# Border of the first two stages of an encoder block: seven weight splits move from VectorE to GpSimd, and the last sixteen tokens' turned tiles share one buffer behind the keys' products

## The reference

```
hn   = rmsnorm(h, attn_norm)
q_g, k_g, v_g, c_q, c_kv, k_r, gates = split(hn @ w_in)      # 512,128,128,384,256,32,2048 columns
q_g  = rope_2d(rmsnorm(q_g per head));  k_g = rope_2d(rmsnorm(k_g per head))
q_m  = rmsnorm(c_q) @ mla_w_uq           # 384 -> 8 heads of 64 + 32 rotated columns
kv   = rmsnorm(c_kv) @ mla_w_ukv         # 256 -> 8 heads of 64 key + 64 value columns
... grouped attention, latent attention, gates, w_out, experts, final norm
```

## Time and profile before

| | us |
|---|---|
| median of 3 runs | 2993.95 (2992.51 to 2995.31) |
| the profiled execution | 2994.37 |
| its span, first to last instruction | 2992.6 |
| TensorE busy in the span | 2826.5 (94%) |
| VectorE, ScalarE, GpSimd busy | 1820.7, 1479.4, 684.4 |

### The profile page before, as it was taken

How to read it: one execution, slowest core, us unless ns; L and a number is a source line. 1 busy time by engine, 2 the same in 40 slices (tenths; PEclk the granted TensorE clock), 3 DMA queues, 4 the chain that set the end, 5 groups by cost and what they waited for, 6 DMA issues and landing times. The chain is left out here.

```text
span 2992.6 us, 56058 instructions
## 1 busy us (share of the span) xinstructions
PE 2826.5 (94%) x20084; PEld 2619.8 (88%) x20084; DVE 1820.7 (61%) x3158; ACT 1479.4 (49%) x2701; POOL 684.4 (23%) x1247
## 2 busy tenths in 40 slices
PE   8999899999999999999999999999965999999994
PEld 7888698999998888887999999988844999999994
DVE  6777767888887777676334334433345555555555
ACT  4333336888887777677223223321222445544443
POOL 0000013444443333334000000000013233332331
PEclk9999898999999999999999999999976999999997
DMA  6556592202113224443757564456655898889977
GB/s 212 158 157 191 152 377 86 71 24 72 50 33 93 75 74 108 102 125 99 225 137 228 160 203 132 144 174 197 190 138 141 198 207 199 201 203 209 207 161 260
DMA packets 529044, 461.87 MB, mean 154 GB/s; under 512 B 53458, under 2 KB 464802, under 8 KB 528880
## 3 DMA queue, kind: packets, MB, share of 16 engines
q1 hardware_dynamic: 510256, 411.74, 48.0%
q0 software_dynamic: 16256, 47.89, 7.5%
q10 hardware_dynamic: 2368, 0.16, 0.0%
HBM read 315.57 MB, written 144.14 MB: 154 GB/s over the span
## 5 line engine op out<-in xcount | busy, mean ns | idle before, releaser
L1576 DVE TENSOR_REDUCE t_peak<-t_s_ps 128x1 f32<-128x1024 f32 (+2 forms) x276 | 336.8, 1221 | 84.8 <-PE t_s_ps L1388 83.9
L1388 PE MATMUL t_s_ps<-t_k,t_q 96*128 96x512 f32 (+2 forms) x1392 | 379.0, 402 | 4.8 <-ACT t_probs L1492 4.8
L1840 PE MATMUL c_acc<-c_tokens,c_w_hi 128*128 128x260 f32 x2048 | 373.0, 283 | 4.5 <-DVE c_w_lo L1913 4.5
L1601 DVE TENSOR_TENSOR t_pt_lo<-t_tp,t_pt_hi 128x512 fp32r<-128x512 f32 x552 | 336.4, 650 | 36.1 <-ACT t_pt_hi L1522 35.5
L1522 ACT CAST t_pt_hi<-t_tp 128x512 fp32r<-128x512 f32 x552 | 284.7, 565 | 113.0 <-PE t_tp L1418 112.0
L1840 PEld LDWEIGHTS c_acc<-c_tokens,c_w_hi 128*128 128x128 f32 x2048 | 316.8, 189 | 4.8 <-issue 4.8
L1492 ACT ACTIVATE t_probs<-t_s_ps,t_bias 128x1024 f32<-128x1024 f32 (+2 forms) x276 | 308.2, 1117 | 22.8 <-POOL t_bias L1655 8.1
L2445 PE MATMUL e_gu<-e_x_hi,w_hi 128*128 128x260 f32 x1024 | 293.7, 287 | 0.9 <-DVE e_x_lo L2650 0.9
L2445 PE MATMUL e_gu<-e_x_lo,w_hi 128*128 128x260 f32 x1024 | 289.9, 283 | 0.0
L1840 PE MATMUL c_acc<-c_tokens,c_w_lo 128*128 128x260 f32 x1024 | 289.8, 283 | 0.0
L2445 PE MATMUL e_gu<-e_x_hi,w_lo 128*128 128x260 f32 x1024 | 289.6, 283 | 0.0
(11 more groups left out here) (299 smaller groups left out, 6569.2 us busy)
## 6 DMA issues: line engine op xcount, KB each, us to landing
c_raw<-in_w_in SPq DMA_DIRECT2D x64, 512.0 KB, 5.6
w_raw<-in_w_gate SPq DMA_DIRECT2D x64, 512.0 KB, 6.9
w_raw<-in_w_up SPq DMA_DIRECT2D x64, 512.0 KB, 9.3
w_raw<-in_w_down SPq DMA_DIRECT2D x64, 512.0 KB, 4.5
c_tokens<-o_t SPq DMA_DIRECT2D x32, 520.0 KB, 6.7
c_tokens<-hn_t SPq DMA_DIRECT2D x16, 1040.0 KB, 9.3
r_mt<-mix_t SPq DMA_DIRECT2D x32, 512.0 KB, 5.2
mix_t<-c_out_hi SPq DMA_DIRECT2D x32, 260.0 KB, 2.1
```

What stands on the lines that cost most here:

```text
L1388: ins = pe.matmul(s_ps[0:r, n % 2, half * 512:(half + 1) * 512], query(n, a), key(n, c, half * 512, (half + 1) * 512), start=(at == 0), st ...
L1576: dve.tensor_reduce(peak[0:r, b % 2, i:i + 1], s_ps[0:r, n % 2, :], AX_X, ALU.max).then_inc(peak_done, 1)
L1601: dve.tensor_tensor(pt_lo[span], tp[:, f % RING, :].rearrange("p (t n) -> p t n", t=4)[:, :, 0:r], pt_hi[span].bitcast(F32), ALU.subtract) ...
L1840: pe.matmul(acc[:, b, mixer, 0:W], w[:, parity, mixer, k, :], tokens[t % 2][:, part, k, cols], start=(k == 0 and at == 0), stop=(k == DK - ...
```

## The change

The pieces of `wq`, `wk` and `wv` (3 + 2 + 2) are split by GpSimd, with a semaphore of their own, `late_piece_lo`; VectorE keeps the three of `wr`. GpSimd's split of the 16 tokens' values, formerly the last round of its loop, now stands behind the seven pieces. The 16 tokens' turned tiles all go into buffer 1 of `a_tp`: heads into its first 16 columns, keys and latents into the next 16, with one signal for both. TensorE turns them behind the keys' products of step 0 instead of before; the keys' products wait only for the turned tiles before (`turned_before`), and the values' products wait for the low parts of the last ones. ScalarE splits step 1's latents behind the 16 tokens' heads (`last_heads_done`) and does its part of the turned tiles (`last_halves`, with seven stores) behind the keys' high part.

```diff
+        LAST_TURNS = fill("qT", N - 1, 0)[0]
+        def spot(kind, s, g):
+            n, b = fill(kind, s, g)
+            if isinstance(s, int) and s == N - 1 and kind != "hnT":
+                return n, 1, META * (n - LAST_TURNS)
+            return n, b, 0
...
-            rest["tensor"] = lambda: body(N, N % 2)
+            def last_turns():
+                pe.wait_ge(post_done, N)
+                at_least(pe, tp_hi, LAST_TURNS)
+                for k in range(HEADS):
+                    pe.transpose(tp[:, 1, k, 0:META], turned[0:META, k, :, :].rearrange("p a b -> p (a b)"),
+                                 ident[0:META, 0:META])
...
+                for k, tile in enumerate(tiles):
+                    ins = pe.transpose(tp[0:tile.shape[-1], 1, k, META:2 * META], tile, ident[0:META, 0:META])
+                ins.then_inc(tp_filled, 2)
+            rest["tensor"] = last_turns
...
             def split_lo(kind, s, g, out_of, hi_of, n_tiles, parts):
-                dve.wait_ge(tp_hi, n + 1)
+                last = isinstance(s, int) and s == N - 1 and kind != "hnT"
+                dve.wait_ge(tp_hi, LAST_TURNS + 2 if last else n + 1)
...
-            steps(pool, body, 1, 1)
+            steps(pool, body, 1, 1, left=1)
+            rest["gpsimd"] = lambda: body(N, N % 2)
...
             def piece_ready(s, w):
                 if s == 0:
-                    pe.wait_ge(piece_lo, pieces_until(w))
+                    if w == 0:
+                        pe.wait_ge(piece_lo, pieces_until(0))
+                    else:
+                        pe.wait_ge(late_piece_lo, pieces_until(w) - pieces_until(0))
...
                 by_columns(s, 0, QRK, wq_hi, wq_lo, blocks(Q, n)).then_inc(q_filled, 1)
                 if s == 0:
-                    projected["rest"]["tensor"]()
-                    pe.wait_ge(*projected["turned"])
+                    pe.wait_ge(*projected["turned_before"])
                 piece_ready(s, 2)
                 at_least(pe, k_lo, s)
                 by_columns(s, QRK, KVRK, wk_hi, wk_lo, blocks(K, n)).then_inc(k_filled, 1)
+                if s == 0:
+                    projected["rest"]["tensor"]()
...
                 piece_ready(s, 3)
+                if s == 0:
+                    pe.wait_ge(*projected["turned"])
...
                 if s == 0:
-                    last_halves()
+                    act.wait_ge(*projected["last_heads_done"])
                     split_latent(1)
                 act.wait_ge(k_filled, s + 1)
                 act.copy(m_hi[p][:, 1, :, 0:n], blocks(K, n)).then_inc(k_hi, 1)
+                if s == 0:
+                    last_halves()
...
             split_latent(0)
-            split_weights((0, 1))
+            split_rotated_weights()
             head_roots()
             last_heads()
...
                 if s == 0:
                     last_halves()
-                    split_weights((2, 3))
...
             pool.wait_ge(*projected["multiplied"])
+            for n, (w, k) in enumerate(PIECES):
+                if w > 0:
+                    pool.wait_ge(piece_hi, n + 1)
+                    pool.tensor_tensor(piece(weights[w][1], k), raw_piece(w, k), piece(weights[w][0], k).bitcast(F32),
+                                       ALU.subtract).then_inc(late_piece_lo, 1)
+            projected["rest"]["gpsimd"]()
```

More of the change, by code:

```diff
@@ L585, in _ @@
             steps(pe, body, 1, 1, left=1)
-            rest["tensor"] = lambda: body(N, N % 2)
+            def last_turns():
[4 more added lines that the diff above has]
+                                 ident[0:META, 0:META])
+                tiles = [turned[0:META, HEADS + h, :, :].rearrange("p a b -> p (a b)") for h in range(KV)] \
+                    + [k_rot[0:META, (N - 1) % 2, :]] + [latent[0:META, k * P:(k + 1) * P] for k in range(QRK + KVRK)]
+                for k, tile in enumerate(tiles):
+                    ins = pe.transpose(tp[0:tile.shape[-1], 1, k, META:2 * META], tile, ident[0:META, 0:META])
+                ins.then_inc(tp_filled, 2)
+            rest["tensor"] = last_turns
         @block.scalar
@@ L598, in copy_hi @@
             def copy_hi(kind, s, g, out_of, n_tiles):
-                n, b = fill(kind, s, g)
+                n, b, at = spot(kind, s, g)
                 r = rows_of(s)
@@ L602, in copy_hi @@
                 if kind == "kcT":
-                    act.copy(lat_st[:, :, 0:r], tp[:, b, KV + 1:, 0:r])
-                act.copy(out_of(r), tp[:, b, 0:n_tiles, 0:r]).then_inc(tp_hi, 1)
+                    act.copy(lat_st[:, :, 0:r], tp[:, b, KV + 1:, at:at + r])
+                act.copy(out_of(r), tp[:, b, 0:n_tiles, at:at + r]).then_inc(tp_hi, 1)
             def body(j, parity, halves=(0, 1)):
@@ L667, in split_lo @@
             def split_lo(kind, s, g, out_of, hi_of, n_tiles, parts):
-                n, b = fill(kind, s, g)
+                n, b, at = spot(kind, s, g)
                 r = rows_of(s)
-                dve.wait_ge(tp_hi, n + 1)
-                dve.tensor_tensor(out_of(r), tp[parts, b, 0:n_tiles, 0:r], hi_of(r).bitcast(F32), ALU.subtract)\
+                last = isinstance(s, int) and s == N - 1 and kind != "hnT"
+                dve.wait_ge(tp_hi, LAST_TURNS + 2 if last else n + 1)
+                dve.tensor_tensor(out_of(r), tp[parts, b, 0:n_tiles, at:at + r], hi_of(r).bitcast(F32), ALU.subtract)\
                     .then_inc(tp_lo, 1)
@@ L800, in body @@
                         .then_inc(v_split, 1)
-            steps(pool, body, 1, 1)
+            steps(pool, body, 1, 1, left=1)
+            rest["gpsimd"] = lambda: body(N, N % 2)
     return dict(rest=rest, multiplied=(proj_filled, N), evacuated=[(proj_act, N), (proj_dve, N)], head_sums=(post_chain, (N - 1) * POST_LINKS + 1),
-                used_table=(post_done, N - 1), turned=(tp_lo, fill("kcT", N - 1, 0)[0] + 1),
+                used_table=(post_done, N - 1), turned=(tp_lo, LAST_TURNS + 2), turned_before=(tp_lo, LAST_TURNS), last_heads_done=(post_done, N),
                 stored=lambda steps_done: (qkv_stored, STORES * steps_done),
@@ L856, in latents @@
         sp_passed, pool_passed = sem("sp_passed"), sem("pool_passed")
-        piece_hi, piece_lo = sem("piece_hi"), sem("piece_lo")
+        piece_hi, piece_lo, late_piece_lo = sem("piece_hi"), sem("piece_lo"), sem("late_piece_lo")
         loaded, lat_split_hi, lat_split_lo = ahead.loaded, sem("lat_split_hi"), sem("lat_split_lo")
@@ L1057, in split_latent, with split_rotated_weights @@
                                       lat_hi[s % 2][:, :, t * P:t * P + r].bitcast(F32), ALU.subtract).then_inc(lat_split_lo, 1)
-            def split_weights(of):
+            def split_rotated_weights():
                 for n, (w, k) in enumerate(PIECES):
-                    if w in of:
+                    if w == 0:
                         dve.wait_ge(piece_hi, n + 1)
```

## The result

The changed kernel is slower. Its median is 3005.2 us (3003.73 to 3007.28, 6 runs) against 2993.34 of the kernel before beside it (2990.68 to 2995.31, 6 runs): a ratio of 1.0035, 95% interval 1.0025 to 1.0045, or 7.5 to 13.5 us. The forecast was 3001.2, on the slow side; 3005.2 lies 0.2 us above the upper end of the range. The profiled execution took 3003.86 us with a span of 3002.1, 9.5 more than the one of before.

A forecast was written before the change was run, and what follows sets the result against it. Bound by the later of two chains meeting at step 3, the one from the 16 tokens' low parts: stall 4.5 + transfers 0.8 + lost clock 2.0 = +7.3 us, median 3001.2 us; 8-in-10 range 2992.5 to 3005.0.

The forecast's parts named there:

- What bounds: Two chains meet at step 3; the later, from the 16 tokens' low parts through SyncE's loads and stores, decides.
- GpSimd's price: Seven subtracts on GpSimd take 8.7 us, about 1.25 each, and cost TensorE nothing to about 1 us.
- VectorE's stall: VectorE waits for GpSimd's subtracts, one instruction through each gap: net +4.5 us (3 to 5.8) on the 16 tokens' heads.
- ScalarE's cover: ScalarE's added wait for the heads costs nothing, with 1 us of cover before VectorE's low parts; without it 1 us more.
- TensorE's step 1: Values' products take 2.9 us, up to 5.8 at half clock; step 1 starts at 356.0 to 358.9 (before: 358.68).
- SyncE: All its work behind the 16 tokens' stores moves 4.5 us with their low parts; first loads at 359.0.
- The stores' landing: Step 0's last store lands later as GpSimd's value stores share full transfer engines: +0.8 us, between 0 and 2.8.
- The clock: TensorE waits 5 us or more before step 3, then runs at half clock: +2.0 us (1.4 to 2.9).
- the two transfer terms: SyncE's stretch from stores to first loads, moved as it was, and step 0's store landing, +0.8 us.
- B: Rival: VectorE's small instructions slip in beside GpSimd without stall, stores decide step 3: +1.0, 2995 us; chance 0.14.
- C: Rival: neither stall nor stores bind, TensorE's step 1 is kept 6 to 9 us earlier: 2986 us; chance 0.08.
- D: Rival: VectorE stalls, but the stores don't bind step 3: -2.8 to +0.2, 2992.7 us; chance 0.12.

The follow-up runs named there:

- e2: The changed kernel, with SyncE loading the first attention unit in step 4 of the second stage instead of ahead of step 0's stores: 2993.14 us, ratio 1.0001.
- e1: The changed kernel, with GpSimd clearing the seven low parts (memset, no reading) instead of subtracting: 2997.91 us, ratio 1.0014 to the kernel before.
- e6: The changed kernel, with each of GpSimd's seven subtracts made twice: 3013.37 us, ratio 1.0058 to the kernel before.
- e4: The changed kernel, with the seven pieces on VectorE (`wv` behind the 16 tokens' low parts), turns still behind the keys' products: 3001.16 us, ratio 1.0020.
- e3: The kernel before, with GpSimd splitting the seven pieces and the 16 tokens still turned ahead of the keys' products: 2999.95 us, ratio 1.0019.
- e5: The changed kernel, with GpSimd clearing instead of subtracting and the first attention unit loaded in step 4: 2989.97 us, ratio 0.9980.

## Why the prediction was right or wrong

*What bounds.* Right: the second chain, from the 16 tokens' low parts over the loads and stores to step 3, decides. e2 cuts it and the loss goes.

*GpSimd's price.* Right: 1.27 us each, 9.0 in all from 331.97 to 340.98 (8.7 was worked out), and TensorE's waits have none for a piece on GpSimd.

*VectorE's stall.* Right in kind and size: one instruction through each gap, a norm not reached before GpSimd was done; low parts 4.7 us late for 4.5. e1 shows that it is the reading subtract, e6 that the stall grows with GpSimd's work. The Trainium skill's sentence on the lock (SBUF — State Buffer, "SBUF: two separate sides") says more than the rows of before could: two-input VectorE instructions meet it only against a GpSimd instruction that reads SBUF, others in a two-port mode against any. e1 agrees with the first half: beside a clear, the two-input links took 0.16 us. It fits the second as far as the one-input L102 and L103, which took 0.48 there, ran in that mode, and no run shows their mode. The rotation, which the prediction let go free, came at 349.0, after GpSimd's end, so nothing here tests that.

*ScalarE's cover.* Right: its copies of the turned tiles ended at 351.2, VectorE came at 352.9. Its seven stores held VectorE up for 2.9 us at line 1137. TensorE did not wait for that; GpSimd's stores of the rotated queries did, and started at 360.27 for 358.97.

*TensorE's step 1.* Right: the values' products ran at 0.50, 5.25 us of a bound of 5.8, and step 1 came where it had been.

*SyncE.* Too small by 0.8. From the first of the 16 tokens' stores to the first load it took 354.49 - 348.84 = 5.65 us before and 360.12 - 353.69 = 6.43 after. The prediction had moved this stretch as it was. It is 6.4 in e1 and e4 too, 6.8 in e6, and 5.65 in e3, so it belongs to the turns' new place; which of its edits does it is not shown, and not all of ScalarE's and SyncE's issues were of their former length (a `kr_t` store took 1.64 us to issue, 0.46 before).

*The stores' landing.* The mis-sized term: +0.8 was taken from 0 to 2.8. From the first load to the landing it took 387.6 - 360.1 = 27.5 us for 379.8 - 354.5 = 25.3: +2.2. GpSimd's value stores had hardly moved (361.95 and 374.68 for 361.74 and 374.28), and step 1's, landed 11.9 us later at 386.6, now lay wholly ahead of the landing. The upper bound was nearer, and the prediction's own argument said so. The other runs fit it: 26.6 to 27.3 us in e1, e3, e4 and e6, with step 1's value store 13 to 17 us behind the first load, where it was 19.8 before. That the store is the cause is argued from this; no run moved it alone.

*The clock.* Right: step 3 to step 4 took 15.0 us for 12.56, so 2.4 for 2.0.

Sum of the terms: 4.7 + 0.8 + 2.2 + 2.4 = 10.1, and step 8 is 10.0 late. With 7.3 the size was 2.8 short, of which 2.2 are the two transfer terms. The medians are 11.9 apart; the last 2 us are within the interval and no stretch of the traces was found for them: behind the start of step 8 the two profiled executions differ by 0.7 in the other direction.

*The rivals.* B, without a stall, was worked out as +1.0; e1, which is that case, gave +4.5 (1.5 to 6.9), since the transfer terms were too small there as well. C needed both links cut; e5 gave 6.1 where it had 6 to 9. D is refuted by the 7.24 us wait at step 3.

## What to carry to other kernels

That GpSimd is idle doesn't make work handed to it free: where VectorE runs a chain of tiny instructions on SBUF, each of them can stand for one whole GpSimd subtract, as the root links did here with one input and with two. So look at what VectorE would be doing in that time, not at how busy it is. Before moving work to shorten a wait, find the next place where the waiting engine meets a second chain: here two chains met within 0.2 us, and 6 us won on one of them were worth nothing until the other was moved. Loads that nobody needs for 100 us don't belong in the queue ahead of stores whose buffers are waited for.

## What the runs showed of the hardware that was not expected

- A one-input `tensor_scalar` of VectorE on 16 partitions and 12 columns stood for a GpSimd clear (0.48 us for 0.16), while two-input instructions beside the same clears didn't (0.16).
- A gap between two GpSimd subtracts let one VectorE link through where the second followed at once (1.21 us each in the changed kernel), and two where it waited for a semaphore first (1.18 and 0.16 in e6).
- With the transfer engines at a share of 0.95, the same 512 KB store took 17.3 us to land behind the unit's loads and 8.7 without them (e2). SyncE's issue of one 8 KB load (L207, at 372.38) took 11.81 us in the changed kernel (7.69 before), beside 0.45 for the 512 KB load ahead of it. The time lies on the issuing queue: step 1's first store, whose low parts were ready at 368.0, was issued behind it at 384.77.
